# RWKV-7 preparation beside HGRN2 projection: one operand tile with whole-row stores, shift work moved, raw tokens requested earlier

## The reference, cut to what matters

```python
def rwkv7_prep(p, p_nb, mu, w0, w_decay2, a0, w_a2, w_g2, k_k, k_a):
    p = p + (p_nb - p) * mu                       # p_nb: mean of the grid neighbours
    r, k, v, lwf, lwb, la, lg = split(p)
    w_logit = stack(w0[0] + tanh(lwf) @ w_decay2[0], w0[1] + tanh(lwb) @ w_decay2[1])
    decay = exp(-RW_DECAY_SCALE * sigmoid(w_logit))
    a = sigmoid(a0 + la @ w_a2)
    g = sigmoid(lg) @ w_g2
    kk = rw_heads(k * k_k)
    kk = kk * rsqrt(maximum(sum(kk * kk, -1, keepdims=True), 1e-12))
    k = rw_heads(k * (1.0 + (a - 1.0) * k_a))

def hgrn2_prep(p, lb):
    q, i, zf, zb, g = split(p, 5)
    z = dir_stack(zf, zb)
    logf = logaddexp(log(lb), log1p(-lb) + log_sigmoid(z))
    k = (1.0 - lb) * sigmoid(-z)
    qs = silu(q)
```

## Time and profile before

| | us |
|---|---|
| median of 3 runs | 5453.29 (5440.58 to 5463.15) |
| the profiled execution, its own time | 5497.27 |
| its span (first to last instruction) | 5495.7 |

### The profile page before, as it was taken

The page is one execution under the profiler, slowest core; times in us unless marked ns, Lnnn a source line. Parts: engine busy times, 40 slices in busy tenths (PEclk is TensorE's granted clock), DMA queues, the critical chain, the costliest instruction groups (busy, mean ns, idle before and its releaser), DMA issues. The chain is left out here.

```text
span 5495.7 us, 117808 instructions
## 1 busy us (share of the span) xinstructions
PE 4415.6 (80%) x44706; PEld 3081.4 (56%) x44706; DVE 2379.1 (43%) x4070; ACT 1179.8 (21%) x3029; POOL 1560.5 (28%) x1933
## 2 busy tenths in 40 slices
PE   3989787878778888888888886778399999999950
PEld 1878655555557878788887875444133333333320
DVE  1121256465655555555555554888211111111138
ACT  0010133333323333333333332222000000000000
POOL 0000011101115555454555543443322222222110
PEclk7999898999888999999999998888699999999985
DMA  9221287878762232323223233432575888998854
GB/s 307 108 75 51 75 171 144 177 140 167 142 139 79 70 84 68 87 68 87 58 64 85 68 87 111 141 124 98 189 296 221 333 355 350 370 373 331 359 237 187
DMA packets 441527, 916.88 MB, mean 167 GB/s; under 512 B 257153, under 2 KB 296449, under 8 KB 408097
## 3 DMA queue, kind: packets, MB, share of 16 engines
q1 hardware_dynamic: 386240, 760.25, 44.4%
q0 software_dynamic: 47392, 133.02, 7.5%
q10 hardware_dynamic: 7488, 17.83, 0.9%
HBM read 951.35 MB, written 211.26 MB: 212 GB/s over the span
## 5 line engine op out<-in xcount | busy, mean ns | idle before, releaser
L2384 PE MATMUL exp_gate_up<-exp_w_gate,exp_rows_and_rowsT 128*64 128x512 f32 x1664 | 760.6, 615 | 93.3 <-DMA exp_w_up<-in_moe_w_up_dram 92.4
L2384 PE MATMUL exp_gate_up<-exp_w_up,exp_rows_and_rowsT 128*64 128x512 f32 x1664 | 761.4, 616 | 0.0
L2384 PEld LDWEIGHTS exp_gate_up<-exp_w_gate,exp_rows_and_rowsT 128*64 128x64 f32 x1664 | 233.1, 142 | 584.5 <-issue 584.3
L1525 POOL TENSOR_TENSOR rw_A_level<-rw_A_rho_beta,const_level_masks 128x256 f32<-128x256 f32 x432 | 342.8, 806 | 749.5 <-DVE rw_A_rho_beta L1541 514.0
L709 PE MATMUL rwp_product<-rwp_hT,rwp_w_rw 128*128 128x256 f32 (+1 forms) x2016 | 443.7, 383 | 0.0
L861 PE MATMUL hgp_product<-hgp_hT,const_w_hg 128*128 128x256 f32 x1728 | 411.3, 395 | 16.0 <-DMA hgp_hT<-s_hT 15.9
L2338 DVE TENSOR_TENSOR exp_hidden<-exp_hidden,exp_gate_up 64x512 f32<-64x512 f32 x104 | 71.9, 692 | 813.0 <-ACT exp_hidden L2319 813.0
L709 PEld LDWEIGHTS rwp_product<-rwp_hT,rwp_w_rw 128*128 128x128 f32 (+1 forms) x2016 | 380.8, 189 | 61.1
L861 PEld LDWEIGHTS hgp_product<-hgp_hT,const_w_hg 128*128 128x128 f32 x1728 | 340.1, 200 | 76.3 <-DMA hgp_hT<-s_hT 16.3
L2408 PE MATMUL exp_down<-exp_w_down,exp_hiddenT 128*64 128x512 f32 x1664 | 380.0, 598 | 1.1
L1556 DVE TENSOR_TENSOR rw_inverse<-rw_inverse,rw_inverse_bank 128x512 f32<-128x512 f32 x288 | 197.7, 686 | 287.5 <-PE rw_inverse_bank L1435 287.5
(11 more groups left out here) (379 smaller groups left out, 8194.0 us busy)
## 6 DMA issues: line engine op xcount, KB each, us to landing
exp_w_gate<-in_moe_w_gate_dram SPq DMA_DIRECT2D x104, 2048.0 KB
exp_w_up<-in_moe_w_up_dram SPq DMA_DIRECT2D x104, 2048.0 KB
exp_w_down<-in_moe_w_down_dram SPq DMA_DIRECT2D x104, 2048.0 KB
rw_operands<-s_rw_in SPq DMA_DIRECT2D x72, 514.0 KB, 5.5
rw_tokens<-s_rw_tm SPq DMA_DIRECT2D x144, 192.0 KB, 6.5
hg_qkf<-s_hg_in SPq DMA_DIRECT2D x36, 768.0 KB, 8.0
mod_w<-in_w_mod_dram SPq DMA_DIRECT2D x24, 1024.0 KB, 26.1
prep_raw<-s_rw_lat SPq DMA_DIRECT2D x16, 1536.0 KB
```

What stands on the lines that cost most here:

```text
L1525: nc.gpsimd.tensor_tensor(self.al[d][l % 2][:], self.ar[u][d][:, :, 0, :], self.K["lvc"][:, d, l, :].unsqueeze(1).broadcast_to([P, NPAIR, ...
L2384: i = nc.tensor.matmul(pgu[u][q:q + BLK], xT[:, k, r * BLK:(r + 1) * BLK], w[r][:, k, :], start=(k == 0), stop=(k == KD - 1))
```

## The change

It does seven things, all in this stage:

1. The q, k and f outputs of the HGRN columns are kept by chunk of 128 tokens, `[P, 2, HH, P]`, so that a store reads 2 KB in a row for each partition instead of four times 512 bytes.
2. The operand tile `w` has the width of the whole DRAM row (1028 floats). DVE writes beta and kappa into it, in the place of a tile `bt` of its own and in place over `pi`.
3. So each chunk and direction is stored with one DMA with 4112 bytes in a row instead of three, two of which had 256 bytes in a row: 4 instead of 12 a half.
4. The two token halves of beta and kappa lie apart now, so PE turns them with plain matmuls against the identity, 64 columns of weights each (128*64), 8 for each of the four uses in a half, where it ran 4 transposes of 128 x 128.
5. The waits of ACT's exponentials for the stores and for PE's turning are gone; DVE waits for both before it writes `w`.
6. SP issues the load of the raw tokens before the stores of the turned tokens.
7. The six passes of `shift` yield 0.28, 0.34, 0.40, 0.46, 0.52, 0.58 instead of 0.05, 0.10, 0.14, 0.34, 0.60, 0.66.

```diff
 class HgProjection
-        self.qo, self.ko, self.fo = (m.sb(f"{x}_out", [P, HH, GROUP]) for x in "qkf")
+        self.qo, self.ko, self.fo = (m.sb(f"{x}_out", [P, 2, HH, P]) for x in "qkf")
...
-                               self.qo[:, :, c * P:(c + 1) * P]).then_inc(s["q_stored"], 16)
+                               self.qo[:, c]).then_inc(s["q_stored"], 16)
...
-                nc.vector.tensor_tensor(self.qo[:, j, :], p[:, 0:GROUP], sig[:, nth % 2, 0, :], ALU.mult).then_inc(s["q_ready"], 1)
+                nc.vector.tensor_tensor(self.qo[:, :, j, :], by_chunk(p[:, 0:GROUP]), by_chunk(sig[:, nth % 2, 0, :]), ALU.mult).then_inc(s["q_ready"], 1)
...
 class RwkvPrep
-        self.w = two("operands", [P, 2, HEAD])
+        self.w = two("operands", [P, 2, ROW])
...
+    def part(self, d, x):
+
+        c0 = x * XW + (NPAIR if x > 1 else 0)
+        return self.w[d][:, :, c0:c0 + XW].rearrange("p c (j t) -> p c j t", t=RW_C)
...
-                sp.dma_start(row_n[:, 0:HEAD], self.w[d][:, c, :]).then_inc(s[f"w_stored{d}"], 16)
-                for x, src in enumerate((self.bt[d], self.pi[d])):
-                    sp.dma_start(row_n[:, HEAD + x * XW:HEAD + (x + 1) * XW].rearrange("p (j t) -> p j t", t=RW_C),
-                                 src[:, :, c * RW_C:(c + 1) * RW_C]).then_inc(s[f"w_stored{d}"], 16)
+                sp.dma_start(row_n, self.w[d][:, c, :]).then_inc(s[f"w_stored{d}"], 16)
+        if ahead:
+            self.load(sp, q + 2)
         for d in range(2):
             sp.wait_ge(s["act_emptied"], ACT_USES * q + 5 + 2 * d + 2)
...
-        if ahead:
-            self.load(sp, q + 2)
         sp.wait_ge(s["b_ready"], q + 1)
...
-            wait(act, s[f"w_stored{d}"], 96 * q)
-            wait(act, s["filled"], N_USES * (q - 1) + 8 + 2 * d)
...
                 for t in range(4):
-                    mm = nc.tensor.transpose(ps[PREP_USES[use][1]][:, t * P:(t + 1) * P], (self.bt, self.pi)[i][d][:, t, :], self.K["ident"][:])
+                    for c in range(2):
+                        mm = nc.tensor.matmul(ps[PREP_USES[use][1]][c * RW_C:(c + 1) * RW_C, t * P:(t + 1) * P], self.part(d, 2 + i)[:, c, t, :],
+                                              self.K["ident"][:], start=True, stop=True)
...
-        yield 0.05
+        yield 0.28
...
-            wait(dve, s[f"w_stored{d}"], 96 * q)
+            wait(dve, s[f"w_stored{d}"], 32 * q)
+            wait(dve, s["filled"], N_USES * (q - 1) + 8 + 2 * d)
...
-            V.tensor_tensor(bt[:], a[:], pi[:], ALU.mult)
-            o.link(V.tensor_tensor(pi[:], k, pi[:], ALU.mult))
+            V.tensor_tensor(out(2), by_chunk(a[:]), by_chunk(pi[:]), ALU.mult)
+            o.link(V.tensor_tensor(out(3), by_chunk(k), by_chunk(pi[:]), ALU.mult))
```

More of the change, by code:

```diff
@@ L775, in z @@
                     pool.dma_start(S["hg_in"][d, bass.ds(n, 1), j].rearrange("n p h t -> p (n h) t"),
-                                   buf[:, :, c * P:(c + 1) * P]).then_inc(s["z_stored"], 16)
+                                   buf[:, c]).then_inc(s["z_stored"], 16)
         z(0)
@@ L811, in dve @@
         nc, s, K, sig = self.nc, self.s, self.K, self.sig
+        by_chunk = lambda t: t.rearrange("p (c t) -> p c t", c=2)
         first = isinstance(g, int) and g == 0
@@ L827, in dve @@
                     dve.wait_ge(s["z_stored"], 128 * g + 64 * d)
-                nc.vector.tensor_scalar(self.ko[:, h, :], sig[:, nth % 2, 0, :], K["omlb"][:, d, h:h + 1], None, ALU.mult)
-                nc.vector.tensor_scalar(self.fo[:, h, :], sig[:, nth % 2, 1, :], K["omlb"][:, d, h:h + 1],
+                nc.vector.tensor_scalar(self.ko[:, :, h, :], by_chunk(sig[:, nth % 2, 0, :]), K["omlb"][:, d, h:h + 1], None, ALU.mult)
+                nc.vector.tensor_scalar(self.fo[:, :, h, :], by_chunk(sig[:, nth % 2, 1, :]), K["omlb"][:, d, h:h + 1],
                                         K["lb"][:, d, h:h + 1], ALU.mult, ALU.add).then_inc(s["k_ready"], 1)
@@ L889, in __init__ @@
         self.a, self.kx, self.t1 = (sb(x, [P, NPAIR, P]) for x in ("a", "kk", "t1"))
-        self.pm, self.pi, self.bt = two("decay", [P, NPAIR, P]), two("inv_decay", [P, NPAIR, P]), two("beta", [P, NPAIR, P])
-        self.w = two("operands", [P, 2, HEAD])
+        self.pm, self.pi = two("decay", [P, NPAIR, P]), two("inv_decay", [P, NPAIR, P])
+        self.w = two("operands", [P, 2, ROW])
         self.tm = two("tokens", [P, 2, D_RW])
@@ L967, in finish @@
     def finish(self, sp):
-        for n, per in (("g_stored", 1), ("v_stored", 4), ("w_stored0", 6), ("w_stored1", 6), ("tm_stored0", 2), ("tm_stored1", 2), ("b_stored", 1)):
+        for n, per in (("g_stored", 1), ("v_stored", 4), ("w_stored0", 2), ("w_stored1", 2), ("tm_stored0", 2), ("tm_stored1", 2), ("b_stored", 1)):
             sp.wait_ge(self.s[n], 16 * per * 2 * NG)
@@ L1116, in shift @@
             o.link(V.tensor_tensor(mix[:], raw[:, :, 0:P], raw[:, :, 2 * GRID_W:], ALU.add))
-            yield 0.10
+            yield 0.34
             o.link(V.tensor_tensor(grid(mix[:], 1, GRID_W), grid(mix[:], 1, GRID_W), grid(own, 0, GRID_W - 1), ALU.add))
-            yield 0.14
+            yield 0.40
             o.link(V.tensor_tensor(grid(mix[:], 0, GRID_W - 1), grid(mix[:], 0, GRID_W - 1), grid(own, 1, GRID_W), ALU.add))
-        yield 0.34
+        yield 0.46
         o.link(V.scalar_tensor_tensor(mix[:], mix[:], scale, own, ALU.mult, ALU.subtract))
-        yield 0.60
+        yield 0.52
         o.link(V.tensor_tensor(mix[:], mix[:], self.mu[:].unsqueeze(2).broadcast_to([P, 14, P]), ALU.mult))
-        yield 0.66
+        yield 0.58
         o.link(V.tensor_tensor(mix[:], mix[:], own, ALU.add))
@@ L1168, in dve @@
             dve.wait_ge(s["decays_ready"], 2 * q + d + 1)
-            wait(dve, s[f"w_stored{d}"], 96 * q)
-            pm, pi, w, bt = self.pm[d], self.pi[d], self.w[d], self.bt[d]
-            out = lambda x: w[:, :, x * XW:(x + 1) * XW].rearrange("p c (j t) -> p c j t", t=RW_C)
+            wait(dve, s[f"w_stored{d}"], 32 * q)
+            wait(dve, s["filled"], N_USES * (q - 1) + 8 + 2 * d)
+            pm, pi, w = self.pm[d], self.pi[d], self.w[d]
+            out = lambda x: self.part(d, x)
             kv, pv, ov = by_chunk(kx[:]), by_chunk(pm[:]), out(0)
@@ L1176, in dve @@
             V.tensor_copy(ov[:, :, :, first], kv[:, :, :, first])
-            V.tensor_copy(w[:, :, 2 * XW:], pv[:, :, :, end])
+            V.tensor_copy(w[:, :, 2 * XW:HEAD], pv[:, :, :, end])
             V.tensor_tensor(out(1), by_chunk(r), pv, ALU.mult)
-            V.tensor_tensor(bt[:], a[:], pi[:], ALU.mult)
-            o.link(V.tensor_tensor(pi[:], k, pi[:], ALU.mult))
+            V.tensor_tensor(out(2), by_chunk(a[:]), by_chunk(pi[:]), ALU.mult)
+            o.link(V.tensor_tensor(out(3), by_chunk(k), by_chunk(pi[:]), ALU.mult))
             dve.sem_inc(s["w_ready"], 1)
```

## The result

The changed kernel takes 5479.78 us (median of 11 runs, 5465.30 to 5483.49); the kernel before, beside it, 5455.31 (11 runs, 5440.58 to 5469.14). The ratio is 1.0041 with a 95% interval of 1.0029 to 1.0054: 22 us slower by this ratio (24.5 by the two medians), where 19 us less were forecast, and outside both the forecast's own range (5418 to 5450) and the wider one (5395 to 5468). The profiled execution of the changed kernel took 5481.12 us itself, like its median. That of before had taken 5497.27, 42 us more than the median that it is compared with here.

The account below looks back on a forecast made before the run. Each half was taken as bound by a chain from PE's decay products over ACT and DVE back to PE. Seven rounds gain 20 us, the first 5, the last loses 6: 5453.3 - 19 = 5434 us, range 5418 to 5450.

Parts of the forecast that it names:

- Both halves: Half A 50.1 us, PE turning 25.3 us after its decay products start (T); half B 56.2 us, turning at T+21.6.
- the place of the q output: In half A on DVE, the q output runs at T+9.2 (T: start of decay products), holding the work behind it.
- the turning block: PE's turning of two uses, 16 matmuls of 128 columns: 1.96 us a block, where 8 transposes took 0.87.
- the request: SP asks for raw tokens at T+37.3 (T: start of decay products), about 4 us after direction 1's operands are ready.
- the absence of the raw wait: DVE's wait for raw tokens falls to near 0 from 138.5 us; they land with 5 us to spare.
- the seven rounds: From half A of the second round to that of the last: 106.3 us a round instead of 109.23, 20 us less.
- the first and the last round: First round 5 us less; last round, with no raw tokens to wait for in half B, 6 us more.
- The clock's price: PE's turning and the product behind it run slower after idling: 2.0 us lost from first block to second.
- the turning runs in pairs: Opposes the rival of serial turning: 3.5 us a block at 0.109 an instruction, 5483 us, chance 0.12.
- the chain is not shorter: Opposes the rival of a shorter chain through DVE: rounds of 100.3 to 102.3 us, 5403 us, chance 0.27.
- the tokens are there in time: Opposes the rival of raw tokens still late: 3 us of wait in each half, 5455 us, chance 0.10.
- the base: The whole kernel's 5453.3 us, from which the 19 us read off the 5497.27 us profiled execution were subtracted unchanged.

Follow-up runs that it names:

- the version with old places: Changed kernel with the six shift passes back at their old places, matmul turning kept: 5391.37 us, ratio 0.988 (chip 11); 5414.26, 0.9827 (chip 1).
- the version with the two last passes early: Changed kernel with old pass places and 4 transposes a use, its last two shift passes moved to 0.52 and 0.58: 5383.49 us, ratio 0.9851 (chip 3).

## Why the prediction was wrong, and where it was right

**The mechanism in the stage held, and most sizes.** Both halves, the place of the q output, the turning block, the request and the absence of the raw wait came within 0.5 us, and the round within 0.4 (106.3 and 105.97). The stage fell by 20.6 where 19 were summed. Two errors in this offset each other: the seven rounds gave 22.8 where 20 were summed, and the first and the last round together cost 2.2 where 1 was summed. The clock's price, 2.0 from block to block, was 2.9 in half A (8.3 less 1.96 and 3.5) and 1.7 in half B; in half A this made PE itself, and not `w_ready`, the last to come: its second block shows no idle time before it. None of the three rivals happened: the turning runs in pairs, the chain is not shorter, and the tokens are there in time. In the single records of the block at 906.58 the two products of a pair start 0.01 us apart and the next pair 0.109 later, which is the pitch that the rival had given to one instruction. The rows of the scans and of the experts together priced the turning rightly (1.96 and 1.97).

**The step that failed is the base**, the sum's last line, "5453.3 - 19 = 5434", and ahead of it "a change worked out in it is taken over to the median unchanged". The profiled execution was 44 us above the median of the runs shown, and I read that as a level that both kernels share. It was not: as far as a trace at the lower level shows, 37 of those us stand in the very wait that the change removes. Where before takes 5455 us its stage is 944.6 and not 981.4, with 126.1 us of waits for raw tokens in it and not 163.2. Who waited for SP's L932, in the trace of the forecast, on chip 1 and on chip 3:

```profile
  DVE prep_mixed L1116: 163.2, 14
...
  DVE prep_mixed L1116: 165.9, 15
...
  DVE prep_mixed L1116: 126.1, 12
```

The changed kernel's 960.8 is the same against both: minus 20.6 against the one, plus 16.2 against the other. With the second base, and the 3.0 us ahead of the scans, the sum would have been 5453.3 + 16.2 + 3.0 = 5472.5, 7 us below what was measured. The sum should have been done for both. The sign was there: the profiled execution lay 0.8% above the median and 34 us above the highest of the three executions, which lay within 0.4%; 29 executions of before on chip 3 lie within 0.5% from lowest to highest.

**How each part of the change pays.** At the new places with cheap turning the stage is the same whatever the stores do: 937.5 (before, only the places changed, chip 11) and 936.9 (all changed, with transposes, chip 3). So on chip 3, with 937 as what the places give:

| kernel | stage | what follows |
|---|---|---|
| before, chip 3 | 944.6 | 126.1 us of raw waits |
| new places, cheap turning | 936.9 | the chain over DVE bounds it: 8 us less |
| the changed kernel | 960.8 | turning by 128*64: 24 us more |
| old places, matmuls (chips 11, 1) | 883.7, 887.1 | 33 us of raw waits |
| old places, transposes (chip 1) | 858.3 | turning back: 29 us less |

My sum had the turning as 1.1 us for the block of direction 1 in half A and twice that in half B, 3.3 us a round; 24 us over nine rounds is 2.7. What it did not ask is what the stage would be if the other edits, the request and the whole-row stores above all, alone shortened the wait. They do: on chip 1 from 165.9 us to 33.0, while the first passes stay at the head of a half, where DVE has little else to do (it waits 95.7 us for ACT's `a` in the changed kernel). Of these, taking back the request alone brings 23 us of waits again, taking back the stores alone 59. The new places put two more passes ahead of direction 0's operands, where PE waits for them. One round of the version with old places, on chip 1, PE's timeline, shows them at T+21.2 and T+17.9 instead of T+25.4 and T+21.7:

```profile
852.43 1.37 PE L1063 MATMUL prep_bank<-prep_tanh_w,prep_low_rank_w 32*128 32x128 f32 x13
...
873.61 3.63 PE L1088 MATMUL prep_bank<-const_ident,prep_operands 128*64 128x128 f32 x32 [2.75 <-DVEq L1185]
...
897.58 1.37 PE L1063 MATMUL prep_bank<-prep_tanh_w,prep_low_rank_w 32*128 32x128 f32 x13
...
915.49 3.68 PE L1088 MATMUL prep_bank<-const_ident,prep_operands 128*64 128x128 f32 x32 [2.97 <-DVEq L1185]
```

So the operands come 4.2 and 3.8 us sooner in a half, 8.0 a round, although the round after this one still waits for raw tokens in half A. The gate product in half A of the second and of the last round gives the mean of seven rounds, (1441.59 - 759.73) / 7 = 97.4 us against 106.0:

```profile
759.73 1.12 PE L1068 MATMUL prep_bank<-prep_gate_w,prep_sig_gate 96*128 96x512 f32 x2
...
1441.59 1.12 PE L1068 MATMUL prep_bank<-prep_gate_w,prep_sig_gate 96*128 96x512 f32 x2
```

That is 8.6 a round, 60 of the 73.8 us by which the two stages differ on that chip (960.9 and 887.1); the first and the last round give the rest. By the version with the two last passes early, these two cost little, so the price lies in the passes ahead of direction 0's operands; they were not moved by themselves. The new places cure a wait that the other edits had mostly cured.

**What stays open.** That the landing differed between the runs on chips 1 and 3 is shown for the same kernel (14.4 and 12.4 us for the token stores); why it did is not. On chip 1 the time of before came out the same in two sets (5512.72 and 5513.41), but chips 3 and 11 had one set each, and what else differed between the sets is not separated from the chip. The chip of the first trace is not known. In this stage it looks like chip 1, by the waits above and by its token stores:

```profile
s_rw_tm<-prep_tokens SPq DMA_DIRECT2D x72, 256.0 KB, 14.0
```

Part of the difference between chips lies elsewhere: of 62.8 us between the spans on chips 1 and 3, 43.1 are this stage and the rest is spread over scans, experts and what lies between. The changed kernel shows it too: 5476.54 and 5492.64 with the same stage.

## What to carry to other kernels

Before a sum is made from one execution, compare its own time with the median; if it is off by more than the executions scatter, work the sum out for a second value of the wait that the change removes, since a wait for small transfers may be the part that differs. A change that removes such a wait may turn its sign from chip to chip, so compare it on more than one. And when several edits aim at one wait, find out which of them suffices: here the cheap ones left 33 us of 166, and moving work into the critical chain on top of them cost 74 us of the stage, net of those 33.

## What the hardware showed that I had not expected

The same kernel took 5455, 5459 and 5513 us on three chips, with the same number of packets in the traces from two of them, while the changed kernel, which after the first load does not wait for raw tokens, had the same stage on two of them within 0.1 us (960.9 and 960.8). The Trainium skill (DMA: Bandwidth & Descriptors, Specifications) says that a transfer under 512 bytes is read, modified and written; here, with 256-byte runs in 12 DMAs against 4112-byte ones in 4 at otherwise equal code, the stage was 945.0 and 887.1 us on one chip where a later load was waited for, and 962.2 and 960.9 where it was not. That small transfers are dear agrees with the rule where somebody waits; no run here shows that they are read, modified and written.

The turning took nearly twice as long behind idle time: 3.6 us against 1.97 in the changed kernel, 1.94 against 1.07 with transposes. The granted clock in three stretches of the changed kernel, the first block, the product behind it and the second block (start and end, length, PE, PEld, DVE, ACT and POOL busy, clock, DMA share, GB/s) is 0.50, the lower level of 1.2 GHz, behind the idle time, 0.77 on average in the product, and 1.00, the upper level of 2.4 GHz, for the second block:

```profile
898.30:901.90 3.60, 3.60 (x33) 3.27 (x33) 3.24 (x3) 0.60 (x1) 0.00 (x0) 0.50 0.74 289
902.00:906.50 4.50, 4.50 (x16) 3.62 (x16) 3.97 (x9) 1.13 (x3) 0.00 (x0) 0.77 0.02 6
906.60:908.50 1.90, 1.90 (x34) 1.73 (x33) 1.72 (x3) 0.60 (x1) 0.00 (x0) 1.00 0.76 305
```
